# Stationary tiles moved to 512-byte multiples, six weight residuals moved to VectorE, and a reordered start, in a two-block transformer kernel

## The reference, cut to what matters

```python
xn = rmsnorm(h, norm_mix_g);  u = xn @ w_in                      # 1024 x 7168
h  = h + (g_a * (attn @ w_attn_out) + g_b * (rnn @ w_rnn_out)) @ w_o
hn = rmsnorm(h, norm_ffn_g)
h  = h + (silu(hn @ w_gate) * (hn @ w_up)) @ w_ffn_out           # 2816 hidden, 3 such layers in all
z  = rms_norm(h, mix_pre_g) @ w_in_2                             # 1024 x 1952
h  = h + rms_norm(mixed @ w_out_2, mix_post_g)
```

## Time and profile before

| what | before |
| --- | --- |
| median of three runs | 1008.18 us |
| the profiled execution, its own time | 1008.32 us |
| its span, first to last instruction | 1006.5 us |
| TensorE busy (matmuls, ends modelled) | 960.4 us, 95% |
| VectorE busy | 499.0 us, 50% |
| ScalarE busy | 491.0 us, 49% |
| GpSimd busy | 355.6 us, 35% |
| 16 DMA queues' mean rate | 168 GB/s |

### The profile page before, as it was taken

How to read it: one execution, slowest core, us unless ns; L and a number is a source line. 1 busy time by engine, 2 the same in 40 slices (tenths; PEclk the granted TensorE clock), 3 DMA queues, 4 the chain that set the end, 5 groups by cost and what they waited for, 6 DMA issues and landing times.

```text
span 1006.5 us, 13874 instructions
## 1 busy us (share of the span) xinstructions
PE 960.4 (95%) x4535; PEld 789.5 (78%) x4535; DVE 499.0 (50%) x831; ACT 491.0 (49%) x771; POOL 355.6 (35%) x178
## 2 busy tenths in 40 slices
PE   6998979999999999999999999997999989999997
PEld 5877767888878888888878888886878768888886
DVE  3329595554445443342663434328478584334322
ACT  5353835664445444443555444436536464444442
POOL 4420000012434444444444434554422344343432
PEclk9999999999999999999999999999999999999999
DMA  6745454444555656769656565554612246665652
GB/s 228 231 153 168 126 187 119 128 143 146 173 162 177 192 175 190 255 212 231 182 170 190 183 187 189 181 159 135 198 55 85 84 134 201 192 183 186 185 180 75
DMA packets 133263, 169.27 MB, mean 168 GB/s; under 512 B 17723, under 2 KB 88926, under 8 KB 133094
## 3 DMA queue, kind: packets, MB, share of 16 engines
q1 hardware_dynamic: 132038, 168.67, 54.9%
q10 hardware_dynamic: 1184, 0.07, 0.1%
HBM read 167.61 MB, written 1.10 MB: 168 GB/s over the span
## 4 chain that ended last, share of the span: by engine, by line
PE 81%; DVE 11%; ACT 4%; issue 3%; DMA 1%; POOL 0%; DVEq 0%; ACTq 0%; POOLq 0%
PE acc L784 24%; PE acc L786 24%; PE acc L785 24%; PE tp L829 4%; DVE w_lo L1159 2%; DVE h L1530 1%; PE sc L902 1%; ACT w_hi L457 1%; DMA gain_x<-in_norm_mix_g 1%; PE acc L1094 1%; DVE u L1245 1%; DVE xt_lo L1540 1%; DVE u L1209 0%; DVE u L1305 0%; ACT xt_hi L685 0%
## 5 line engine op out<-in xcount | busy, mean ns | idle before, releaser
L457 ACT ACTIVATE w_hi<-w_raw 128x1024 fp32r<-128x1024 f32 x305 | 322.0, 1060 | 386.7 <-PE acc L786 356.7
L1754 POOL TENSOR_TENSOR w_lo<-w_raw,w_hi 128x1024 fp32r<-128x1024 f32 x132 | 321.0, 2432 | 437.3 <-ACT w_hi L457 437.3
L1159 DVE TENSOR_TENSOR w_lo<-w_raw,w_hi 128x1024 fp32r<-128x1024 f32 x173 | 223.2, 1297 | 342.8 <-ACT w_hi L457 341.2
L784 PE MATMUL acc<-w_hi,xt_hi 128*128 128x512 f32 (+1 forms) x880 | 351.5, 399 | 5.3 <-DVE w_lo L1159 3.4
L786 PE MATMUL acc<-w_lo,xt_hi 128*128 128x512 f32 (+1 forms) x880 | 343.9, 391 | 0.0
L785 PE MATMUL acc<-w_hi,xt_lo 128*128 128x512 f32 (+1 forms) x880 | 343.4, 390 | 0.0
L784 PEld LDWEIGHTS acc<-w_hi,xt_hi 128*128 128x128 f32 x880 | 166.3, 189 | 41.2 <-DVE w_lo L1159 4.7
L786 PEld LDWEIGHTS acc<-w_lo,xt_hi 128*128 128x128 f32 x880 | 166.1, 189 | 34.9
L785 PEld LDWEIGHTS acc<-w_hi,xt_lo 128*128 128x128 f32 x880 | 166.5, 189 | 32.4
L784 PE MATMUL acc<-w_hi,hid_hi 128*128 128x512 f32 x264 | 105.0, 398 | 0.0
L785 PE MATMUL acc<-w_hi,hid_lo 128*128 128x512 f32 x264 | 104.6, 396 | 0.0
(11 more groups left out here) (192 smaller groups left out, 804.4 us busy)
## 6 DMA issues: line engine op xcount, KB each, us to landing
w_raw<-in_ffn_w_gu SPq DMA_DIRECT2D x176, 256.0 KB
w_raw<-in_w_in SPq DMA_DIRECT2D x68, 512.0 KB
w_raw<-in_w_ffn_in SPq DMA_DIRECT2D x88, 256.0 KB
w_raw<-in_ffn_w_down SPq DMA_DIRECT2D x44, 512.0 KB
w_raw<-in_w_ffn_out SPq DMA_DIRECT2D x22, 512.0 KB
w_raw<-in_w_rnn_out SPq DMA_DIRECT2D x8, 512.0 KB
w_raw<-in_w_attn_out SPq DMA_DIRECT2D x8, 512.0 KB
w_raw<-in_w_o SPq DMA_DIRECT2D x8, 512.0 KB
```

The lines of the kernel that those rows point to most:

```text
L457: act.activation(w_hi[:, b, :], w_raw[:, b, :], ACT.Copy).then_inc(hi_done[b], 1)
L784: pe.matmul(o, hi[:, k, rows], wh, start=first and n == 0, stop=False)
L1159: dve.tensor_tensor(w_lo[:, b, :], w_raw[:, b, :], w_hi[:, b, :].bitcast(F32), ALU.subtract).then_inc(lo_done[b], 1)
L1754: pool.tensor_tensor(w_lo[:, b, :], w_raw[:, b, :], w_hi[:, b, :].bitcast(F32), ALU.subtract).then_inc(lo_done[b], 1)
```

## The change

It has four parts.

1. **Addresses.** `top` begins at 16896 = 33 x 512, `base` is rounded up to a multiple of 512, and tiles of 2048 bytes or more behind it to a multiple of 64. After it `w_raw`, `w_hi`, `w_lo`, `h` and all eight tiles of activation pairs start at multiples of 512 bytes.
2. **Residuals.** `lo_on_dve` also gives VectorE slabs 0 to 3, 212 to 215 and 235 to 242 whole. That takes slabs 1 and 3, 213 and 215, and 235, 237, 239 and 241 from GpSimd.
3. **x in three pieces.** Columns 0 to 255, 256 to 511 and 512 to 1023 of both row tiles, issued ahead of slabs 0, 1 and 2. TensorE transposes two column blocks from each of the first two, and the rest behind slabs 0 and 1 of the first group. The gains come as 8 rows of 512 bytes; TensorE transposes them into `sc[0]`, and VectorE copies them to `gain_x`.
4. **Products of zeros.** TensorE multiplies zeros by zeros four times at the start and once behind each of the first two transposes. The loop over the first four groups is written out.

```diff
--- before.py
+++ after.py
@@ -106,12 +106,14 @@
 
 def build(nc, a, out):
 
-    top = [16512]
+    top = [16896]
 
     def place(name, shape, dt, at=None):
         size = int(np.prod(shape[1:])) * (2 if dt == BF16 else 4)
         size = (size + 31) // 32 * 32
         if at is None:
+            if size >= 2048:
+                top[0] = (top[0] + 63) // 64 * 64
             at = top[0]
             top[0] += size
         return nc.alloc_sbuf_tensor_at(name, shape, dt, offset=at)
@@ -137,7 +139,7 @@
     coef = place("coef", [P, 8, MT], F32)
     minus_half = place("minus_half", [P, MT], F32)
     junk = place("junk", [P, D], BF16)
-    base = top[0]
+    base = top[0] = (top[0] + 511) // 512 * 512
 
 
     u = place("u", [P, 7, MT, D], F32)
@@ -156,6 +158,7 @@
     pt1 = place("pt1", [P, 2, 384], F32)
     ext_sb = nc.alloc_sbuf_tensor_at("ext_sb", [HEADS, 384], F32, offset=top[0] - size_of(2, 384))
     mx1 = place("mx1", [P, 2, 4], F32)
+    gain_rows = sb1[0:KT, 1, 0:P]
     carrier = place("carrier", [P, 8], F32)
     free_marks = place("free_marks", [P, 8], F32)
     nm1 = place("nm1", [P, 2, 4], F32)
@@ -229,8 +232,10 @@
     tp_free = [sem(f"tp_free{b}") for b in range(2)]
     hi_written = sem("hi_written")
     ssq_done, ms_done, rs_done = sem("ssq_done"), sem("ms_done"), sem("rs_done")
-    x_landed = [sem("x_landed0"), sem("x_landed1")]
-    ident_landed, gain_x_landed, par_landed = sem("ident_landed"), sem("gain_x_landed"), sem("par_landed")
+    x_landed = [sem(f"x_landed{c}") for c in range(3)]
+    ident_landed, par_landed = sem("ident_landed"), sem("par_landed")
+    gain_rows_landed, gain_turned, gain_x_ready = sem("gain_rows_landed"), sem("gain_turned"), sem("gain_x_ready")
+    zero_ready = sem("zero_ready")
     bd_zero, bd_landed, q_zero = sem("bd_zero"), sem("bd_landed"), sem("q_zero")
     merge_landed = sem("merge_landed")
     table_landed, ext_done, ext_stored = sem("table_landed"), sem("ext_done"), sem("ext_stored")
@@ -263,7 +268,7 @@
 
     def lo_on_dve(q):
 
-        return q % 2 == 0 or 20 <= q < 60
+        return q % 2 == 0 or q < 4 or 20 <= q < 60 or S["in2"] <= q < S["in2"] + 4 or S["out2"] + 4 <= q < S["f3i"] + 4
 
     def n_of(n, i=0, per=0):
 
@@ -347,11 +352,11 @@
                         after[n]()
 
             xv = a["x"].rearrange("b (m p) d -> p (b m) d", p=P)
-            sp.dma_start(h[:, 0, :], xv[:, 0, :]).then_inc(x_landed[0], 16)
-            sp.dma_start(h[:, 1, :], xv[:, 1, :]).then_inc(x_landed[1], 16)
             w_in = a["w_in"][0]
-
             for q in range(4):
+                if q < 3:
+                    cols = (slice(0, 256), slice(256, 512), slice(512, D))[q]
+                    sp.dma_start(h[:, :, cols], xv[:, :, cols]).then_inc(x_landed[q], 16)
                 slab(q, rect(q, w_in, 256 * q, 3 * D))
 
             for name, key in (("mix_g", "norm_mix_g"), ("ffn_g", "norm_ffn_g"), ("fin_g", "final_norm_g"),
@@ -475,18 +480,15 @@
 
 
             act.dma_start(ident[:], a["c_ident"]).then_inc(ident_landed, 16)
-            with nc.allow_non_contiguous_dma(reason="a column of gains"):
-                act.dma_start(gain_x[:], a["norm_mix_g"][0].rearrange("(k p) -> p k", p=P)).then_inc(gain_x_landed, 16)
+            act.dma_start(gain_rows, a["norm_mix_g"][0].rearrange("(k p) -> k p", p=P)).then_inc(gain_rows_landed, 16)
 
 
             act.wait_ge(set_up, 1)
             act.activation(junk[:, 0:MT], minus_half[:], ACT.Exp).then_inc(warm, 1)
-            act.wait_ge(gain_x_landed, 16)
+            act.wait_ge(gain_x_ready, 1)
             for n in range(4):
                 split(X["x"] + n, (2 * n, 2 * n + 1), gain_x, xt_hi)
-                if n > 0:
-                    feed(n - 1, 1)
-            feed(3, 1)
+                feed(n, 1)
             for m in range(MT):
                 square("x", 0, m, h[:, m, :])
 
@@ -841,16 +843,28 @@
             XT, YT, HID = (xt_hi, xt_lo), (yt_hi, yt_lo), (hid_hi, hid_lo)
 
 
+            def over_zeros(n):
+
+                for _ in range(n):
+                    pe.matmul(sc[1][:, 0:T], sb1[:, 0, 0:P], sb1[:, 0, 0:T], start=True, stop=True)
+
+            def turn_x(n):
+                pe.wait_ge(x_landed[min(n, 2)], 16)
+                turn_tiles(X["x"] + n, h, (2 * n, 2 * n + 1))
+
+            pe.wait_ge(zero_ready, 1)
+            over_zeros(4)
             pe.wait_ge(ident_landed, 16)
-            for m in range(MT):
-                pe.wait_ge(x_landed[m], 16)
-            for n in range(4):
-                turn_tiles(X["x"] + n, h, (2 * n, 2 * n + 1))
-
-            ready = pairs_ready(X["x"])
-            with pe.Fori(0, 2) as i:
-                for g in range(2):
-                    group(4 * g, g, XT, 4, i, 2, 1, ready=ready)
+            pe.wait_ge(gain_rows_landed, 16)
+            pe.transpose(sc[0][:, 0:KT], gain_rows, ident[0:KT, 0:KT]).then_inc(gain_turned, 1)
+            turn_x(0)
+            over_zeros(1)
+            turn_x(1)
+            over_zeros(1)
+
+            group(0, 0, XT, 4, ready=pairs_ready(X["x"]), after={0: lambda: turn_x(2), 1: lambda: turn_x(3)})
+            for g in range(1, 4):
+                group(4 * g, g, XT, 4)
 
             def turn_xr_gr(tile_pairs):
                 for g in range(4):
@@ -1184,6 +1198,7 @@
                                   ALU.add).then_inc(ms_done, 1)
 
 
+            dve.memset(sb1[:, 0, 0:T], 0.0).then_inc(zero_ready, 1)
             dve.memset(minus_half[:], -0.5).then_inc(set_up, 1)
 
             dve.memset(carrier[:], 0.0).then_inc(o_drained, 2)
@@ -1192,11 +1207,12 @@
             dve.memset(free_marks[:, 4:5], 0.0).then_inc(ttr_done, 1)
             dve.memset(xrT[:, :, 0:3], 0.0).then_inc(set_up, 1)
             dve.memset(bias1[0:CHUNK, :, :, 0:CHUNK], MASKED).then_inc(set_up, 1)
+            dve.wait_ge(gain_turned, 1)
+            dve.tensor_copy(gain_x[:], sc[0][:, 0:KT]).then_inc(gain_x_ready, 1)
+            dve.wait_ge(gain_x_ready, 1)
             for n in range(4):
                 split(X["x"] + n, (2 * n, 2 * n + 1), gain_x, xt_hi, xt_lo, HI["x"] + 2 * n)
-                if n == 1:
-                    feed(0, 2)
-            feed(2, 2)
+                feed(n, 1)
             mean_square("x")
 
             def pcol(name, n=KT, off=0):
@@ -1550,7 +1566,7 @@
             for m in range(MT):
                 mean_square("f2", m)
                 gained("f2", G["f2o"] + 1, 1, 1, S["f2o"] + 21, (m,))
-                feed(S["in2"] + 2 * m, 1)
+                feed(S["in2"] + 2 * m, 2)
                 for g in (G["f2o"], G["f2o"] + 1):
                     wait_drained(dve, g, m)
                 add_normed("f2", m, h_new, lambda m, c: f[:, m, c * W:(c + 1) * W])
```

## The result

The changed kernel takes 997.78 us (median of 4 runs, 994.14 to 998.59), the kernel before beside it on the same chip 1008.25 us (1007.77 to 1008.45). The ratio is 0.9887, with a 95% interval of 0.9869 to 0.9904. It is faster by 10.5 us, where 45.3 were forecast: the median lies 0.2 us inside the range and 35 us from the number. On another chip the changed kernel took 998.01 us against 1008.42 (0.9908, 0.9884 to 0.9932). The profiled execution shown here took 994.14 us, its span is 992.4.

The account below looks back on a forecast made before the run. TensorE's pace of starting products was taken as the bound (three product lines, 72.8%). 42.0 + 3.0 + 1.3 - 0.8 = 45.5 us off 1008.3 gave 962.8, said as 963 us; own range 956 to 971, with the distance case 955 to 998.

Parts of the forecast that it names:

- Addresses, 42.0 us: All products on TensorE's chain fall to 216 ns once both operands start at multiples of 512: 42.0 us gained.
- a line through the two measured points: Product pitch against stationary address, 226.7 ns at 128 bytes and 234.3 at 224, extended to 216.5 ns at zero.
- The second support: Four float32 matmuls of 256 columns, taken as 512 steps without surplus, at 215 ns each: lower bound of the pitch.
- The term for `xt`, 23.3 us: 2180 products with `xt` stationary, at 128 bytes, gain 10.7 ns each: 23.3 us.
- the 18.7 us for the rest: 1020 products on `hid`, `yt` or `c`, at 224 bytes, gain 18.3 ns each: 18.7 us.
- the first rival: Only the distance between both operands counts: `xt` stays at 226.7 ns, the rest join it, 7.8 us; 996 us, chance 0.22.
- the line at 215: Bound on the address gain with products at 215 ns: 46 us.
- The row that warned: 15 products of 416 columns on `xt` at 189.3 ns, surplus 16, put down to moving address or operand distance.
- The port rule: TensorE's two read ports make weight loads free, so stationary addresses could not matter and the address gain would be nothing.
- The start, 3.0 us: First product at 9.7 us, 3.7 us sooner, 0.7 given back in the first group: 3.0 us; bounds 1 and 5.
- The residuals, 1.3 us: In the transitions, three additions to `h` gain 2.1 us each, four VectorE residuals cost 1.2 each: 1.3 us taken.
- New waits, 0.8 us: Where VectorE is already late, a faster TensorE comes earlier to the same wait: 0.8 us lost.

Follow-up runs that it names:

- pitch_map: Kernel of TensorE alone, series of 48 float32r products at many stationary/moving addresses (bytes past a multiple of 512): 226.65 ns at 0/0, 234.6 at 224/128.
- the maps: Three kernels that compute nothing of the reference, series of 48 products at varied operand addresses, widths and types: float32r of 512 columns from 226.65 ns, bf16 215.8.
- resid_only: Kernel before with only slabs 213, 215, 235, 237, 239 and 241 split by VectorE: 1008.65 us against 1009.72, ratio 0.9993.
- old_resid: Changed kernel with GpSimd making slabs 213, 215, 235, 237, 239 and 241 again: 1000.08 us, 2.1 us over the changed kernel.
- trans: Changed kernel with VectorE's order of residuals and additions changed in the two transitions, slab 241 GpSimd's again: 995.80 us, 0.9868 of the kernel before.

## Why the prediction was wrong, step by step

**Addresses, 42.0 us: the step that failed.** It is "a line through the two measured points ... meets zero at 216.5 ns", with 216 ns then taken for all 3200 products on the chain. The line had no ground: the pitch isn't a function of the stationary residue. `pitch_map` has 128/128 and 0/0 at the same 226.65 ns, and 228.7 at 192/0 beside 234.6 at 96/0. The second support, that float32 matmuls of 256 columns take 215, was misread and of another kind: the four instructions that I counted in the earlier trace rows are two matmuls of two records each, and 215.8 is half of one. bf16 of 512 columns does run at 215.8, float32r does not go under 226.65. Two numbers that agreed within 1.5 ns measured two different things. The term for `xt`, 23.3 us, was nothing; of the 18.7 us for the rest the first rival kept 7.8, and 4.9 were measured. So 42.0 us became 4.9. (The sum for the line at 215 is 45 us, not 46.)

That rival, with its condition (only the distance counts), its price (7.8 us) and its sum (996 us), is what happened, within 1.8 us of the median. I gave it 0.22, "nothing ties the line's meeting point to 216" being the reason against it. The row that warned, 416 columns with a surplus of 16 ns where 512 have 13.3, was seen and put down to the moving address: `pitch_map` has 188.3 ns there at 0/0 too, 15 over the columns. A surplus that doesn't shrink with the columns says that a part of it is fixed.

Its 7.8 us came out as 4.9 and 4.8. A clean piece is the third feed-forward layer, from the first transposes of `hid` to the last matmul, before and after:

```profile
830.27 0.65 PE L829 MATMUL tp<-ident,hid 128*128 128x128 f32 x4 [0.32 <-DVE hid L1452]
...
1000.37 0.40 PE L786 MATMUL acc<-w_lo,hid_hi 128*128 128x512 f32 x1
```
```profile
817.90 0.65 PE L831 MATMUL tp<-ident,hid 128*128 128x128 f32 x4 [0.29 <-DVE hid L1468]
...
986.22 0.39 PE L788 MATMUL acc<-w_lo,hid_hi 128*128 128x512 f32 x1
```

170.10 against 168.32 us, 1.78 us for 264 products, 6.7 ns each and not 7.6: behind each set of transposes the pitch moves between 224 and 236 ns for some 4 to 18 products before it settles at 226.7. Three layers give 5.3 us. The remaining products at the old residue, 192 on `yt` and 36 on `c`, lie beside waits, where I take a faster product to gain little. This is read from traces, not tested apart; and since the clock differs by 0.001 to 0.01 from run to run, a part of the gap between 7.8 and 4.9 us can be the clock's.

**The port rule.** The prediction set the trace against the page "TensorE: Matmul & The Clock Gate" of the Trainium skill (section "Part 2: What happens when you issue a matmul": two read ports, so that the next weights take nothing from the running matmul). For bf16 the maps agree with it, 215.8 ns at the four places tried. For float32r they do not: the distance of the two addresses moves the pitch by up to 7.9 ns. With a block of 64 columns or fewer they do not either way. What the two operands share was not shown.

**The start, 3.0 us: right in size, 3.5 measured.** The first product was forecast at 9.7 us and came at 8.76. The turned gains and the first four transposes were ready for `xt_hi` at 5.66 us, where I had 6.4 from landings of larger transfers. The eight products at the high clock, which I had only as a bound, were there and are worth 1.4 us in the trace. What I called given back is larger than the 0.7 us that I took: from the start of a slab's last product to the start of the next slab's first are 0.6 and 0.8 us behind slabs 0 and 1 (four transposes in each) and again 0.6 and 0.8 behind slabs 2 and 3, in place of 0.23. The second stage's first transposes come 3.8 us sooner, so of 4.6 us at the first product and 1.4 by the clock some 2.2 were given back. That the size came out is in part luck: the 1.4 that I left out and the 1.5 that I took too little nearly cancel. A product of zeros is 0.43 us and not the 0.2 that I took; both single ones ran where TensorE would have waited anyway.

**The residuals, 1.3 us: not contradicted.** `resid_only` gives 1.1 and `old_resid` 2.1 us, neither told from the other nor from nothing; the waits at the transitions say 1.7 and 0.4. The additions fell as said. At `f2` a residual of 1.2 us ahead of the addition against 2.1 us gained is about what the waits show. At the last `mix` I had 1.2 us for each residual, and there the pair ahead of `xt_lo`, and the pair at 800.27, keep TensorE 1.3 and 2.3 us where the same two waits were 0.4 and 0.3; 3.4 us of waits for `h` went for it. `trans` took 1.2 of the 4.0 us there back.

**New waits, 0.8 us.** Not tested: it was to come from a faster TensorE, and `xt` did not get faster. Between 71 and 162 us the waits did not grow as the prediction has it: its three over 2 us were 2.69, 2.17 and 2.72 and are 2.70, 2.18 and 2.72; one of 1.15 us, for ScalarE, is new.

**Range and chances.** 955 to 998 held the median of 997.78 with 0.2 us to spare, because it reached to the rival; on the other chip the median was 998.01, just outside. That it held is luck as much as the rival. The weight was wrong: 0.55 on an extrapolation beyond both measured points, 0.22 on the value that needed none.

## What to carry to other kernels

A pitch read at two places bounds nothing beyond them: for a forecast below the best pitch in the trace, look for one instruction of the same kind that runs there, and if there is none, take the best pitch seen as the likeliest. For float32r products, keep the stationary and the moving operand a multiple of 256 bytes apart and both at multiples of 32; a common offset does as well as alignment. When two engines' work is exchanged to shorten one instruction, ask what else now stands in the same engine's row in front of the next wait.
